# Layer b's projection: gates beside z columns, last weights in a used buffer, sample preparation and position part moved into other stages

## The chip, the core and the metric

The kernel runs on one core of a Trainium2 chip. TensorE (PE; its weight loads are PEld), VectorE (DVE), ScalarE (ACT) and GpSimd (POOL) each run an instruction list written for them and meet at semaphores; SyncE (SP) issues the DMA transfers. The metric is device microseconds of one launch: 1354.34 us before, the median of 3 runs (1353.39 to 1355.47).

## The reference, cut to what matters

The model is a decoder step of two layers, a (dilated attention) and b (native sparse attention), for 512 prompt tokens and 8 x 4 = 32 sample tokens. The change lies in layer b's projection and in the compression of the prompt's keys and values:

```python
def project_b(h, w_in, q_gain, k_gain, pos):
    u = jnp.einsum('ntd,de->nte', h, w_in)          # 1024 -> 3632 columns
    q = rms_norm(u[..., :WIDTH_B]..., q_gain)       # 1024 columns
    kv = u[..., WIDTH_B:o1]...                      # 1536 columns
    gates = jax.nn.sigmoid(u[..., o1:o1 + 3 * HEADS_B]...)   # 48 columns
    z = u[..., o1 + 3 * HEADS_B:]                   # 1024 columns

def compress_rows(x, pe, w1, w2):
    proj = jnp.einsum('ncjkd,rjde->rncke', chunks, w1r)
    hid = jnp.einsum('jd,jde->e', pe, w1)           # the position part: one vector of 128 for k, one for v
    for r in range(CMP_RATIO):
        hid = hid + proj[r, :, r:r + n_cmp]
    return jnp.einsum('ncke,ed->nckd', jax.nn.silu(hid), w2)
```

All data is float32; a matmul of the kernel stands in the trace as two PE instructions.

## The kernel before, in words

A stage is a block: each engine has its list, and the next stage starts when all five lists, SP's among them, are through and a barrier has passed. Layer b runs norm, `project_b_stage`, `prepare_sample_b_stage`, `compress_prompt_stage`, `attend_b_stage`, then the samples.

`project_b_stage` goes through `cols`, eight groups c of weight columns: 0 and 1 are q, 2 to 4 keys and values, 5 the 48 gate columns, 6 and 7 z. For each group there are five units: four tiles of 128 prompt tokens, and the 32 samples. A prompt unit is 8 matmuls over K (L1247), with the tokens as the 128-wide weights and the group's columns streamed. A sample unit (L1244) packs four 32-wide weight loads side by side on the array, each with a quarter of the columns; the gate group has its samples in one plain pass of 32 rows. Units rotate over three PSUM banks; ACT and DVE take them out. After the unit three later, `turn` (L1218 to L1224) transposes a unit's q or keys.

The weights have two slots in `W`: group c lies in slot c % 2, and SP loads group c + 2 when group c is through (L1178). Behind each such load SP issues two copies of sample caches from HBM to HBM (L221), 1 MB and 4 MB. `plain` and `rot` hold normed and rotated q until they are transposed; after group 1 nothing uses them. After group 6, SP issues the weights of the compression (L1577 to L1581) into slot 0.

`prepare_sample_b_stage` then copies the samples' q into a padded tile `T.q` (L1966, 64 small copies on DVE, after POOL cleared it), their keys, values and z into `T` (ACT), stores the samples' gates to HBM and loads them back in another layout (L1911, L1921: eight transfers of 4-byte elements), loads the prompt's key and value rows back as pages (L1916, into slot 1), and computes the position part: 32 matmuls with 128-wide weights from `w1` and a single streamed column (L1938), of which DVE copies the result to `pe_hid` (L1971).

`compress_prompt_stage` works in steps. PE transposes pages (`turn`, L1424), DVE and ACT copy half of each out, then 16 matmuls (`hidden`, L1439, four quarters between the next transposes), SiLU with `pe_hid` as bias (`silu`, L1503), the second weights (`tokens`, L1454) and a norm of the keys. There is one PSUM bank for `turn`, so each waits for both copies of the one before, and one for `hidden`: its second half waits for the first half's SiLU.

Of the kernel before, what the change touches and what calls it, by code (L numbers as in the profile page):

```python
# [13 lines left out]
P = 128  # L14
# [42 lines left out]
def constants():  # L57
# [61 lines left out]
    for name, a in parts.items():  # L119
# [8 lines left out]
            "pa_w0", "pa_w1", "pb_w0", "pb_w1", "cmp_w", "cp_pages0", "cs_pages0", "cs_pages1", "oa_w", "ob_w"]  # L128
# [993 lines left out]
def project_b_stage(S, hT, W, QP, KT, ROWS, WINR, Z, GATES, T_rows, T_z, weights):  # L1122
# [8 lines left out]
    cols = [(0, 512), (512, 512), (1024, 512), (1536, 512), (2048, 512), (2560, NG), (2560 + NG, 512), (3072 + NG, 512)]  # L1131
    NC = len(cols)
    units = []
    for c in range(NC):
        for t in range(TILES + 1):
# [7 lines left out]
            u.R = (2 * NS if u.kv else NS if c == 5 else P) if u.s else P  # L1143
# [3 lines left out]
    with ExitStack() as ctx:  # L1147
# [10 lines left out]
        plain = sb("plain", [P, 3, 512])  # L1158
        rot = sb("rotated", [P, 3, 512])
        s_w = [S.lasting_sem(f"pb_w{i}") for i in range(2)]  # L1160
# [8 lines left out]
        with S.block() as block:  # L1169
            @block.sync  # L1170
            def _(sp):
                for i, name in enumerate(("b_q_norm", "b_k_norm")):
                    sp.dma_start(gains[:, i, :], A[name].broadcast_to((P, DH))).then_inc(s_gains, 16)
                for c in range(NC):
                    if c + 2 < NC:
                        lo, n = cols[c + 2]
                        sp.wait_ge(s_u, 5 * (c + 1))
                        sp.dma_start(W[:, c % 2, :, 0:n], w[:, :, lo:lo + n]).then_inc(s_w[c % 2], 16)  # L1178
                        copy_kept(S, sp, 3, [c])
                        copy_kept(S, sp, 2, [c])  # L1180
# [21 lines left out]
                S.outs += [(S.s_rows_out, 64), (s_win_out, 64), (s_srows_out, 12 * 16)]  # L1202
                sp.wait_ge(s_u, 5 * (NC - 1))
                load_compress_weights(S, sp, weights)

            @block.tensor
            def _(pe):
# [18 lines left out]

                def columns(u, k, j):
                    w_k = W[:, u.c % 2, k, :]
                    if u.kv:
                        return w_k[:, j * P:(j + 1) * P]  # L1230
                    return w_k.rearrange("p (k g d) -> p g k d", k=2, g=GQA)[:, j]
                for u in units:
                    n = cols[u.c][1]
                    if u.t == 0:
                        pe.wait_ge(s_w[u.c % 2], 16 * (u.c // 2 + 1))
                    if u.v >= 3:
                        old = units[u.v - 3]
                        pe.wait_ge(s_n if old.qk else s_lin, old.i + 1)
                        if old.kv:
                            pe.wait_ge(s_v, old.i - 9)  # L1240
                    for k in range(KC):
                        if u.s and u.c != 5:
                            for j in range(4):
                                ins = nc.tensor.matmul(U[u.v % 3][j * NS:(j + 1) * NS, 0:P], hT[:, k, SEQ:TOK], columns(u, k, j),  # L1244
                                                       start=(k == 0), stop=(k == KC - 1), skip_group_check=True)
                        else:
                            ins = nc.tensor.matmul(U[u.v % 3][0:u.R, 0:n], hT[:, k, u.t * P:u.t * P + u.R], W[:, u.c % 2, k, 0:n],  # L1247
                                                   start=(k == 0), stop=(k == KC - 1))
                    ins.then_inc(s_u, 1)
# [4 lines left out]
            def _(act):  # L1254
# [12 lines left out]
                for u in units:  # L1267
# [14 lines left out]
                    elif u.c == 5:  # L1282
                        nc.scalar.activation(GATES[0:u.R, u.t, :], src[0:u.R, 0:n], ACT.Sigmoid).then_inc(s_lin, 1)
                    else:
                        dst = Z[:, u.t % TILES, (u.c - 6) * 512:(u.c - 5) * 512]
                        if u.s:
                            nc.scalar.activation(T_z[:, u.c - 6, :], src[:, 0:P], ACT.Silu).then_inc(s_lin, 1)
                        else:
                            nc.scalar.activation(dst.rearrange("p (g k d) -> p k g d", g=GQA, d=DH),
                                                 src[:, :].rearrange("p (k g d) -> p k g d", g=GQA, d=DH), ACT.Silu).then_inc(s_lin, 1)  # L1290
# [4 lines left out]
            def _(pool):  # L1295
                for u in qk_units:
# [29 lines left out]
            def _(dve):  # L1326
# [45 lines left out]
                second(qk_units[-1])  # L1372

# [520 lines left out]
def prepare_sample_b_stage(S, QP, KT, T_rows, T_z, GATES, T, weights, pages):  # L1894

    nc, A = S.nc, S.dram  # L1900
# [637 lines left out]
```

## Time and profile before

| | us |
|---|---|
| median of 3 runs | 1354.34 |
| profiled execution: its own time | 1350.71 |
| profiled execution: span, first to last instruction | 1348.9 |
| PE busy in the span | 1222.2 (91%) |
| projection of layer b, gate group, four prompt tiles and samples | 722.3 to 735.5 |
| projection, two z groups | 735.5 to 796.1 |
| preparation of the samples, with the position part | 796.1 to 812.1 |
| compression of the prompt | 812.1 to 835.4 |

Times in the trace are counted from the start of the span. In rows of the timeline the columns are start, duration from the first start to the last end of the merged instructions, engine, line, operation, output and inputs, count, and in brackets the idle time just before and what ended it. In tables by stretch, PEclk is the granted TensorE clock: 1.00 is 2.4 GHz, 0.50 is 1.2 GHz.

### The profile page before, as it was taken

What the parts mean: (1) busy time and instruction counts of PE and PEld (TensorE: products, weight loads), DVE (VectorE), ACT (ScalarE), POOL (GpSimd) and SP (SyncE); (2) the same over time, 40 slices, a digit from 0 to 9 for tenths busy, and PEclk for the clock granted to TensorE, in tenths of its full rate; (3) what the DMA queues carried; (4) which work ended last, traced back from release to release, by engine and by line L of the source; (5) the groups of instructions that cost most, each with busy time, mean ns of one, the idle gap of its engine ahead of it and who ended that gap; (6) DMA issues with size and microseconds to landing.
All of it is one profiled execution on the core that took longest, in us unless ns stands there. A gap on an engine that the chain in (4) does not pass through costs nothing. (4 is left out here: it accounts for less than half of the span.)

```text
span 1348.9 us, 20946 instructions
## 1 busy us (share of the span) xinstructions
PE 1222.2 (91%) x7869; PEld 792.6 (59%) x7869; DVE 463.0 (34%) x1205; ACT 394.1 (29%) x947; POOL 295.5 (22%) x423
## 2 busy tenths in 40 slices
PE   3999999999898889699999997999988879797898
PEld 2576576677687743355446465565557767585543
DVE  1333333000455521244121013666742343434321
ACT  5111111111566400512112013666643333333210
POOL 1455554000000000167232001554530000000000
PEclk9999999999999989799998986999989989898999
DMA  6034334582312996336677932302026847343801
GB/s 234 30 147 165 158 136 180 195 290 98 99 44 80 303 295 182 127 125 218 244 230 283 297 55 73 112 2 63 1 58 177 203 125 189 116 135 99 214 9 59
DMA packets 87646, 197.21 MB, mean 146 GB/s; under 512 B 9770, under 2 KB 39258, under 8 KB 86394
## 3 DMA queue, kind: packets, MB, share of 16 engines
q1 hardware_dynamic: 87546, 195.87, 45.7%
q8 instruction: 63, 1.03, 0.3%
q14 instruction: 37, 0.30, 0.1%
HBM read 185.16 MB, written 73.28 MB: 192 GB/s over the span
## 5 line engine op out<-in xcount | busy, mean ns | idle before, releaser
L446 PE MATMUL bank<-la_region,la_hT 128*128 128x512 f32 x640 | 283.2, 599 | 1.7 <-PEq L164 1.7
L446 PEld LDWEIGHTS bank<-la_region,la_hT 128*128 128x128 f32 x640 | 173.1, 275 | 96.2 <-issue 46.7
L1247 PE MATMUL bank<-lb_region,lb_oT 128*128 128x512 f32 (+2 forms) x528 | 210.2, 558 | 2.1 <-PEq L164 1.7
L1247 PEld LDWEIGHTS bank<-lb_region,lb_oT 128*128 128x128 f32 (+1 forms) x528 | 96.5, 199 | 104.4 <-issue 103.3
L1439 PE MATMUL bank<-cs_chunks_turned,lb_region 128*128 128x252 f32 x512 | 125.9, 392 | 4.7 <-ACT cs_hidden L1503 3.9
L1439 PEld LDWEIGHTS bank<-cs_chunks_turned,lb_region 128*128 128x128 f32 x512 | 96.0, 197 | 18.9 <-issue 5.7
L1492 DVE COPY cs_chunks_turned<-bank 64x512 f32<-64x512 f32 x64 | 43.7, 683 | 97.1 <-PE bank L1424 97.1
L1494 ACT ACTIVATE cs_chunks_turned<-bank 64x512 f32<-64x512 f32 x64 | 38.0, 593 | 114.4 <-PE bank L1424 114.3
L494 POOL TENSOR_TENSOR pa_swapped<-pa_normed,pa_tables 128x256 f32<-128x256 f32 (+1 forms) x60 | 50.2, 856 | 77.3 <-DVE pa_normed L513 77.3
L1828 POOL TENSOR_SCALAR ab_probs<-ab_probs,ab_rec,lb_gates 128x128 f32<-128x128 f32 (+3 forms) x96 | 58.2, 623 | 33.8 <-DVE ab_rec L1874 33.6
L465 ACT ACTIVATE pa_squares<-bank 128x512 f32<-128x512 f32 (+1 forms) x30 | 16.0, 533 | 162.4 <-PE bank L446 154.8
L1535 POOL TENSOR_SCALAR cs_ms<-cs_ss 63x4 f32<-63x4 f32 x8 | 1.5, 186 | 252.7 <-DVE cs_ss L1546 252.7
L2233 PE MATMUL bank<-lb_region,lb_oT 128*128 128x512 f32 x128 | 55.9, 595 | 0.0
L1723 PE MATMUL bank<-lb_kT,lb_qp 64*128 64x512 f32 (+3 forms) x256 | 53.6, 497 | 1.4 <-PEq L164 1.1
L1798 ACT ACTIVATE ab_probs<-ab_probs,ab_low 128x128 f32<-128x128 f32 (+3 forms) x96 | 52.6, 551 | 0.0
L484 POOL TENSOR_TENSOR pa_rstd<-pa_mean_square,consts 128x8 f32<-128x8 f32 (+1 forms) x30 | 51.0, 1699 | 2.5
L1275 ACT ACTIVATE pb_squares<-bank 128x256 f32<-128x256 f32 (+3 forms) x25 | 10.8, 431 | 130.6 <-PE bank L1247 125.3
L1860 DVE CUSTOM_DVE_ANT_0 ab_probs<-bank,consts 128x128 f32<-128x128 f32 (+3 forms) x96 | 43.0, 486 | 16.6 <-PE bank L1723 16.6
L687 POOL TENSOR_TENSOR la_z<-la_z,aa_rec 128x512 f32<-128x512 f32 x4 | 4.2, 1043 | 187.7 <-DVE aa_rec L702 187.7
L505 DVE TENSOR_REDUCE pa_square_sum<-pa_squares 128x8 f32<-128x512 f32 (+1 forms) x30 | 18.1, 603 | 72.7 <-ACT pa_squares L465 72.7
L2233 PEld LDWEIGHTS bank<-lb_region,lb_oT 128*128 128x128 f32 x128 | 24.0, 190 | 30.2 <-issue 30.2
L1676 ACT ACTIVATE lb_region<-bank 128x512 f32<-128x512 f32 (+3 forms) x64 | 27.8, 434 | 47.1 <-PE bank L1734 46.9
(334 smaller groups left out, 1808.1 us busy)
## 6 DMA issues: line engine op xcount, KB each, us to landing
la_region<-in_a_w_in SPq DMA_DIRECT2D x10, 2048.0 KB, 8.0
out_new_dil_s<-in_cache_dil SPq DMA_DIRECT2D x8, 2032.0 KB, 13.5
lb_region<-in_b_w_in SPq DMA_DIRECT2D x7, 2048.0 KB, 9.0
la_region<-in_cache_dil SPq DMA_DIRECT2D x13, 1024.0 KB, 15.8
lb_qp<-in_cache_nsa_paged SPq DMA_DIRECT2D x32, 256.0 KB, 4.7
lb_region<-in_cache_nsa_paged SPq DMA_DIRECT2D x32, 256.0 KB, 4.0
sb_sel_keys<-in_cache_nsa_paged SPq DMA_DIRECT2D x64, 128.0 KB, 3.8
sb_sel_values<-in_cache_nsa_paged SPq DMA_DIRECT2D x64, 128.0 KB, 4.1
```

What stands on the lines that cost most here:

```text
L446: ins = nc.tensor.matmul(U[u.v % 3][:, :], permuted(hT[:, k, :], u.g, u.t), W[:, u.c % 2, k, :], start=(k == 0), stop=(k == KC - 1))
L484: nc.gpsimd.tensor_tensor(rstd[:, i % 2, 0:H], ms[:, 0:H], S.const("half_power")[:, 0:H], ALU.pow).then_inc(s_rstd, 1)
L494: nc.gpsimd.tensor_tensor(o3[:, :, lo:lo + HALF], n3[:, :, HALF - lo:DH - lo], tab, ALU.mult).then_inc(s_sw, 1)
L1247: ins = nc.tensor.matmul(U[u.v % 3][0:u.R, 0:n], hT[:, k, u.t * P:u.t * P + u.R], W[:, u.c % 2, k, 0:n], start=(k == 0), stop=(k == KC - 1))
L1439: ins = nc.tensor.matmul(self.hid_bank[:, 0:KVH * nb], self.w1[:, kv, off, mm, :], self.chunksT[:, y % 2, :, mm, off:off + nb], start=(rm ...
L1492: nc.vector.tensor_copy(dst, src).then_inc(self.s_ev[0], 1)
L1494: nc.scalar.activation(dst, src, ACT.Copy).then_inc(self.s_ev[1], 1)
L1723: nc.tensor.matmul(SC[u][:, 0:b.N], QP[b.j][part, 1, g, own_q], KT[part, 1 if b.win else 0, b.j, 0:b.N], start=True, stop=True).then_inc(s ...
L1798: nc.scalar.activation(slots[i][:, 0:b.N], slots[i][:, 0:b.N], ACT.Exp, bias=low[:, i:i + 1], scale=-1.0, accum_out=den[:, i:i + 1]).then_ ...
L1828: nc.gpsimd.tensor_scalar(slots[i][:, 0:b.N], slots[i][:, 0:b.N], rec[:, i:i + 1], GATES[:, b.t, at:at + 1], ALU.mult, ALU.mult).then_inc( ...
L1860: nc.vector.tensor_tensor_reduce(slots[i][:, 0:b.N], SC[u][:, 0:b.N], S.const("causal")[:, (TILES - 1 - b.t) * P:], -SCALE, 3e38, ALU.add, ...
L2233: ins = nc.tensor.matmul(B[6 + v % 2][:, :], oT[:, k, t * P:(t + 1) * P], W_out[:, k, half * 512:half * 512 + 512], start=(k == 0), stop=( ...
```

## The change

The gate group takes the first 256 z columns with it (304 columns), group 6 has 512 z columns, group 7 the last 256. Group 7's weights (1 MB) go into the memory of `plain` and `rot`, which are now one tile, and are issued with group 5's, two groups earlier than before. Slot 1 is thus free after group 5, and the pages are loaded into it from there. The preparation stage is gone: clearing of `T.q`, its copies, the copies of keys and values, and the round trip of the gates stand in the projection's lists; the transposes of z and the position part stand in the compression's. The position part now has the 32-wide broadcast column as weights and streams `w1`'s 128 columns, for k and v side by side on the array; the result lies in rows and is copied, transposed and copied again.

```diff
-    cols = [(0, 512), (512, 512), (1024, 512), (1536, 512), (2048, 512), (2560, NG), (2560 + NG, 512), (3072 + NG, 512)]
+    cols = [(0, 512), (512, 512), (1024, 512), (1536, 512), (2048, 512), (2560, NG + 256), (2816 + NG, 512), (3328 + NG, 256)]
...
+        both = sb("plain_and_rotated", [P, 6, 512])
+        plain, rot = both[:, 0:3, :], both[:, 3:6, :]
+        W_last = both[:, 0:4, :].rearrange("p a b -> p (a b)").rearrange("p (k e) -> p k e", k=KC)
...
+                        if c + 2 < NC - 1:
+                            lo, n = cols[c + 2]
+                            sp.dma_start(W[:, c % 2, :, 0:n], w[:, :, lo:lo + n]).then_inc(s_w[c % 2], 16)
+                        if c == 3:
+                            lo, n = cols[NC - 1]
+                            sp.wait_ge(s_tr, 10)
+                            sp.dma_start(W_last[:, :, :], w[:, :, lo:lo + n]).then_inc(s_w_last, 16)
...
+                sp.wait_ge(s_u, 5 * (NC - 2))
+                sp.wait_ge(S.s_rows_out, 16 * TILES)
...
+                    sp.dma_start(pages0[lo:lo + 64, b // 2, :, :], rows[b, :, :, 0:512]).then_inc(S.lasting_sem("cp_pages0"), 16)
+                sp.wait_ge(s_lin, 5)
+                sp.dma_start(A["scratch_gates"], GATES[0:NS, TILES, :]).then_inc(s_gs, 16)
                 sp.wait_ge(s_u, 5 * (NC - 1))
                 load_compress_weights(S, sp, weights)
+                sp.wait_ge(s_gs, 16)
...
+                        sp.dma_start(T.gates[64 * n2:64 * n2 + 64, pair, :],
+                                     A["scratch_gates"][r:r + NT].rearrange("t (b h) -> h t b", b=3),
+                                     allow_slow_non_contiguous=True).then_inc(s_gl, 16)
+                sp.wait_ge(s_gl, 16 * NB)
...
+                    if u.s and u.c == 5:
+                        for k in range(KC):
+                            ins = nc.tensor.matmul(U[u.v % 3][0:NS, P:P + NG], hT[:, k, SEQ:TOK], weight_rows(u, k)[:, 0:NG],
+                                                   start=(k == 0), stop=(k == KC - 1), skip_group_check=True)
...
+                        functions = ["gates"] * (u.c == 5) + ["z"]
+                        for f in functions if u.t % 2 == 0 else functions[::-1]:
...
+                    if u.c == 6 and u.s:
+                        act.wait_ge(s_ev, 20)
+                        nc.scalar.activation(T.kT[:, :, :, :], KT[:, :, :, SEQ:TOK], ACT.Copy)
...
+                nc.gpsimd.memset(T.q[:, :, :, :, :, :, :], 0.0).then_inc(s_zero, 1)
...
+                                nc.vector.tensor_copy(T.q[part, var, n, j, k2, :, :],
+                                                      QP[j][part, var, :, SEQ + n * NT:SEQ + (n + 1) * NT]).then_inc(s_q, 1)
+                dve.wait_ge(s_q, 8 * NB)
...
-def prepare_sample_b_stage(S, QP, KT, T_rows, T_z, GATES, T, weights, pages):
...
+                for j in range(2):
+                    ins = nc.tensor.transpose(ZB[:, j * P:(j + 1) * P], T_z[:, j * P:(j + 1) * P], ident)
+                ins.then_inc(s_zt, 1)
+                pe.wait_ge(S.lasting_sem("cmp_w"), 16 * 8)
+                nc.tensor.transpose(PB[:, 0:32], pe_rows[:, :], ident[0:32, 0:32])
+                nc.tensor.transpose(PB[:, 128:256], gains[:, :, :].rearrange("p a d -> p (a d)"), ident).then_inc(s_pet, 1)
+                C.pe_step(pe, 0)
+                pe.wait_ge(s_petc, 2)
+                for rm in range(16):
+                    for kv in range(2):
+                        ins = nc.tensor.matmul(HB_[kv * NS:(kv + 1) * NS, 0:HID], peT[:, 16 * kv + rm:16 * kv + rm + 1].broadcast_to((P, NS)),
+                                               w1[:, kv, rm // 8, rm % 8, :], start=(rm == 0), stop=(rm == 15), skip_group_check=True)
+                ins.then_inc(s_ph, 1)
+                C.pe_step(pe, 1)
+                pe.wait_ge(s_phc, 1)
+                nc.tensor.transpose(ZB[:, 256:256 + 2 * NS], hid_rows[:, :], ident[0:2 * NS, 0:2 * NS]).then_inc(s_pht, 1)
...
+                for x in range(4, 8):
+                    C.copy_out(act, x, 1)
+                act.wait_ge(s_pre, 1)
+                C.silu(act, 0)
...
+                C.dve_step(dve, 0)
+                dve.wait_ge(s_ph, 1)
+                nc.vector.tensor_copy(hid_rows[:, :], HB_[0:2 * NS, 0:HID]).then_inc(s_phc, 1)
+                C.dve_step(dve, 1)
+                dve.wait_ge(s_pht, 1)
+                nc.vector.tensor_copy(pe_hid[:, :], ZB[:, 256:256 + 2 * NS:NS]).then_inc(s_pre, 1)
```

SP's list from the last cache copies of the projection (`out_new_win_s`, `out_new_dil_s`) to the end of the preparation; `in_b_cmp_w` is the compression's weights, `out_new_rows_p` into `lb_region` the pages, `lb_s_gates` the samples' gates. Before:

```order
99 L221 DMA out_new_win_s<-in_cache_nsa_win 16x16256
100 L221 DMA out_new_dil_s<-in_cache_dil 64x16384
101 L1577 DMA lb_region<-in_b_cmp_w 64x16x128 x4
102 L1578 DMA lb_w<-in_b_cmp_w 128x2x64
103 L1579 DMA lb_pe_rows<-in_b_cmp_pe 32x128
104 L1581 DMA lb_k_gains<-in_b_k_norm 128x64 x2
105 L160 UNCONDITIONAL_BRANCH
106 L1909 UNCONDITIONAL_BRANCH
107 L1911 DMA scratch_gates<-lb_gates 32x48
108 L1916 DMA lb_region<-out_new_rows_p 64x2x512 x4
109 L1921 DMA lb_s_gates<-scratch_gates 64x3x1 x8
```

And now:

```order
99 L221 DMA out_new_win_s<-in_cache_nsa_win 16x16256
100 L221 DMA out_new_dil_s<-in_cache_dil 64x16384
101 L1215 DMA lb_region<-out_new_rows_p 64x2x512 x4
102 L1217 DMA scratch_gates<-lb_gates 32x48
103 L1642 DMA lb_region<-in_b_cmp_w 64x16x128 x4
104 L1643 DMA lb_w<-in_b_cmp_w 128x2x64
105 L1644 DMA lb_pe_rows<-in_b_cmp_pe 32x128
106 L1646 DMA lb_k_gains<-in_b_k_norm 128x64 x2
107 L1224 DMA lb_s_gates<-scratch_gates 64x3x1 x8
108 L160 UNCONDITIONAL_BRANCH
```

The pages and the store of the gates moved ahead of the compression's weights; the eight loads of the gates stand behind them, at the end of the projection's list (the branch ends a stage's list).

PE's list from the last groups of the projection into the compression; a x8 row is one prompt unit (8 matmuls), the 32-wide rows are the samples. Before, from the gate group on:

```order
297 L1247 MATMUL bank<-lb_region,lb_oT 128x48 x8
298 L1247 MATMUL bank<-lb_region,lb_oT 32x48 x8
299 L1247 MATMUL bank<-lb_region,lb_oT 128x512 x32
300 L1244 MATMUL bank<-lb_region,lb_oT 32x128 x32
301 L1247 MATMUL bank<-lb_region,lb_oT 128x512 x32
302 L1244 MATMUL bank<-lb_region,lb_oT 32x128 x32
303 L160 UNCONDITIONAL_BRANCH
304 L1926 UNCONDITIONAL_BRANCH
305 L1929 MATMUL bank<-consts,lb_s_z 128x128 x2
306 L1933 MATMUL bank<-consts,lb_pe_rows 128x32
307 L1934 MATMUL bank<-consts,lb_k_gains 128x128
308 L1938 MATMUL bank<-lb_peT,lb_region 128x1 x32
```

And now, from the last z groups on:

```order
292 L1282 MATMUL bank<-pb_plain_and_rotated,lb_oT 128x256 x32
293 L1279 MATMUL bank<-pb_plain_and_rotated,lb_oT 32x64 x32
294 L160 UNCONDITIONAL_BRANCH
295 L2400 UNCONDITIONAL_BRANCH
296 L2404 MATMUL bank<-consts,lb_s_z 128x128 x2
297 L2407 MATMUL bank<-consts,lb_pe_rows 128x32
298 L2408 MATMUL bank<-consts,lb_k_gains 128x128
299 L1489 MATMUL bank<-consts,lb_region 128x128 x8
300 L2413 MATMUL bank<-lb_region,lb_peT 32x128 x32
301 L1504 MATMUL bank<-cp_chunks_turned,lb_region 128x124 x4
```

One stage's end is gone, group 7 streams half as many columns, and the position part (L2413) stands between the first four transposes of pages (L1489, two pages each) and the first quarter of `hidden` (L1504).

## Rows read from the trace of the kernel before

**Rows 1.** Table by stretch of all engines; columns: stretch, length, busy times (instructions), PEclk, DMA.

```profile
core 0: us, PE busy (x) PEld busy (x) DVE busy (x) ACT busy (x) POOL busy (x), PEclk, DMA share, GB/s
722.30:735.50 13.20, 12.83 (x88) 12.05 (x87) 2.77 (x8) 3.95 (x12) 4.16 (x9) 0.70 1.09 397
...
766.10:796.10 30.00, 29.65 (x132) 13.76 (x128) 0.00 (x0) 2.95 (x6) 0.00 (x0) 1.00 0.46 75
796.10:812.10 16.00, 13.58 (x69) 13.15 (x69) 6.08 (x67) 1.80 (x6) 0.95 (x1) 0.60 0.34 68
812.10:835.40 23.30, 15.64 (x98) 13.44 (x99) 4.44 (x11) 4.53 (x13) 1.21 (x3) 0.72 0.00 1
```

**Rows 2.** Timeline, PE: sample units, gate units, a quarter of the samples' hidden part.

```profile
720.25 1.69 PEld L1244 LDWEIGHTS bank<-lb_region,lb_oT 128*32 128x32 f32 x64 [0.17 <-issue]
...
724.42 1.99 PE L1247 MATMUL bank<-lb_region,lb_oT 128*128 128x48 f32 x16
...
727.01 3.12 PE L1247 MATMUL bank<-lb_region,lb_oT 128*128 128x48 f32 x16 [0.37 <-DVE pb_normed L1344]
...
793.80 1.95 PE L1244 MATMUL bank<-lb_region,lb_oT 128*32 128x128 f32 x64
...
1055.69 1.87 PE L1439 MATMUL bank<-cs_chunks_turned,lb_region 128*128 128x252 f32 x8
```

**Rows 3.** Table by stretch of all engines, cut where the granted clock changes.

```profile
727.60:737.40 9.80, 9.80 (x49) 8.35 (x49) 0.28 (x1) 2.13 (x5) 0.13 (x1) 0.50 1.05 392
...
796.00:798.40 2.40, 1.16 (x7) 0.79 (x7) 0.62 (x8) 1.57 (x7) 0.95 (x1) 1.00 0.02 3
798.40:822.60 24.20, 20.68 (x97) 19.14 (x97) 7.96 (x67) 2.60 (x8) 0.00 (x0) 0.52 0.22 45
822.60:833.50 10.90, 7.00 (x64) 6.37 (x62) 1.66 (x4) 1.98 (x6) 1.19 (x2) 0.97 0.01 2
```

**Rows 4.** Timeline of the preparation stage.

```profile
797.95 5.97 DVE L1966 COPY lb_s_q<-lb_qp 64x16 f32<-64x16 f32 x64
...
798.09 12.72 PE L1938 MATMUL bank<-lb_peT,lb_region 128*128 128x1 f32 x64 [0.35 <-DVE lb_k_gain L1958]
...
799.77 6.47 SPq L1921 DMA_DIRECT2D lb_s_gates<-scratch_gates  x8
810.92 0.16 DVE L1971 COPY lb_pe_hidden<-bank 128x2 f32<-128x2 f32 x1 [7.00 <-PE bank L1938]
```

**Rows 5.** Timeline of the compression stage.

```profile
812.09 0.66 PE L1424 MATMUL bank<-consts,lb_region 128*128 128x128 f32 x2 [1.28 <-PEq L164]
...
816.97 2.04 PE L1439 MATMUL bank<-cp_chunks_turned,lb_region 128*128 128x124 f32 x8 [0.56 <-DVE cp_chunks_turned L1492]
...
823.35 1.05 PE L1439 MATMUL bank<-cp_chunks_turned,lb_region 128*128 128x124 f32 x8
...
834.33 0.28 DVE L1558 TENSOR_SCALAR lb_kc_p<-bank,lb_k_gain 128x62 f32<-128x62 f32 x1 [1.73 <-PE bank L1464]
```

**Rows 6.** Timeline, SP's issues at the projection's end.

```profile
735.90 9.07 SPq L221 DMA_DIRECT2D out_new_win_s<-in_cache_nsa_win  x1
...
766.26 6.01 SPq L1577 DMA_DIRECT2D lb_region<-in_b_cmp_w  x4
...
775.83 0.90 SPq L1581 DMA_DIRECT2D lb_k_gains<-in_b_k_norm  x2
```

**Rows 7.** SP's waits, 560 to 840; columns: total us, times, longest.

```profile
SPq L160 <- DMA lb_s_gates<-scratch_gates: 1.8, 1, 1.8
```

**Rows 8.** Table by stretch of the DMA engines; columns: stretch, length, PEclk, DMA share, GB/s.

```profile
718.00:722.20 4.20, 1.00 0.02 4
722.20:764.50 42.30, 0.88 1.02 370
...
768.00:780.00 12.00, 1.00 1.12 184
```

**Rows 9.** DMA issues, 722 to 722.6: count, KB, us from issue to landing.

```profile
lb_region<-in_b_w_in SPq DMA_DIRECT2D x1, 2048.0 KB, 7.8
```

More of the change, by code:

```diff
@@ L1142, in project_b_stage @@
             u.heads = (2 if u.s else 8) if u.q else (2 if u.s else 4)
-            u.R = (2 * NS if u.kv else NS if c == 5 else P) if u.s else P
+            u.R = 2 * NS if u.s and u.kv else P
             u.ri = u.i if c < 2 else u.i - 5
@@ new lines, in _ @@
+                    if u.c == 6 and u.s:
+                        act.wait_ge(s_ev, 20)
+                        nc.scalar.activation(T.kT[:, :, :, :], KT[:, :, :, SEQ:TOK], ACT.Copy)
+                        act.wait_ge(s_v, 15)
+                        for which in range(2):
+                            for j in range(2):
+                                nc.scalar.activation(T.v[:, which, j * P:(j + 1) * P], T_rows[(2 + j) * NS:(3 + j) * NS, 1 + which, :],
+                                                     ACT.Copy)
@@ L1372, in _ @@
                 second(qk_units[-1])
+                dve.wait_ge(s_zero, 1)
+                dve.wait_ge(s_ev, 10)
+                for var in range(2):
+                    for j in range(2):
+                        for k2 in range(2):
+                            part = slice(k2 * DH, (k2 + 1) * DH)
+                            for n in range(NB):
+                                nc.vector.tensor_copy(T.q[part, var, n, j, k2, :, :],
+                                                      QP[j][part, var, :, SEQ + n * NT:SEQ + (n + 1) * NT]).then_inc(s_q, 1)
+                dve.wait_ge(s_q, 8 * NB)
 class Compress:
@@ L2398, in _, with compress_prompt_stage @@
                 interleave((scores, least, weights, turns, output, merge), lambda y: C.dve_step(dve, y), unit, rest)
-def compress_prompt_stage(S, KC_P, VC_P, weights, pages):
+def compress_prompt_stage(S, KC_P, VC_P, weights, pages, T_z, T):
+    nc = S.nc
     s_pg = [S.lasting_sem("cp_pages0")]
+    w1, _, pe_rows, peT, pe_hid, gains, gain = weights
+    s_zt, s_pet, s_petc, s_ph, s_phc, s_pht, s_pre = (
+        S.sem("pp_" + n) for n in ("z_turned", "turned", "copied", "hidden", "hidden_copied", "hidden_turned", "hidden_done"))
+    ZB, PB, HB_ = S.banks[3:6]
     def landed(pe, it, s_pg):
@@ L2415, in _ @@
             def _(act):
-                for y in range(C.last):
+                act.wait_ge(s_zt, 1)
+                nc.scalar.activation(T.zT[:, :], ZB[:, 0:2 * P], ACT.Copy)
+                C.act_step(act, 0)
+                for x in range(4, 8):
+                    C.copy_out(act, x, 1)
+                act.wait_ge(s_pre, 1)
+                C.silu(act, 0)
+                for y in range(2, C.last):
                     C.act_step(act, y)
@@ L2424, in _ @@
             def _(dve):
-                for y in range(C.last):
+                dve.wait_ge(s_pet, 1)
+                nc.vector.tensor_copy(peT[:, :], PB[:, 0:32]).then_inc(s_petc, 1)
+                nc.vector.tensor_copy(gain[:, :], PB[:, 128:129]).then_inc(s_petc, 1)
+                C.dve_step(dve, 0)
[4 more added lines that the diff above has]
+                nc.vector.tensor_copy(pe_hid[:, :], ZB[:, 256:256 + 2 * NS:NS]).then_inc(s_pre, 1)
+                for y in range(2, C.last):
                     C.dve_step(dve, y)
```

142 lines of the change are left out of this document (47 added, 95 removed).

## The prediction

> **What bounds the kernel now.** I read the table by stretch first [rows 1], cut at the stages that the change touches. In the z groups PE is busy 29.65 of 30.00 us at the full clock (1.00, 2.4 GHz), so there only fewer or shorter PE instructions help. The gate group before them takes 13.20 us at a mean clock of 0.70, though it streams a tenth of the columns. The preparation stage takes 16.00 us and the compression 23.30 us, at 0.60 and 0.72. Nothing of another stage lies beside them, since each stage ends at a barrier, so what leaves this stretch leaves the total, unless another list of the same stage ends late.
>
> Second, the timeline of these stages. A gate unit of 16 instructions takes 1.99 us at the full clock, 0.12 us for one, and 3.12 us where the clock has fallen [rows 2]; the clock stood at 0.50 (1.2 GHz) from 727.6 to 737.4, after some 5 us of these short units, and came back in the 512-column units that followed [rows 3]. In the preparation PE's 64 one-column instructions (798.09 to 810.81) are the longest list and DVE's copy at 810.92 waits for them; DVE's 64 copies and SP's eight gate loads lie beside them [rows 4]. SP's list ends 1.8 us after its last gate issue [rows 7], at 808.1, so it was nearly as late. In the compression the clock is still at 0.52 until 822.6 [rows 3].
>
> **The change, part by part.** The profiled execution took 1350.71 us (span 1348.9), the median of the runs is 1354.34; I sum in the trace's time and take the difference off the median.
>
> *The three groups.* A 512-column instruction costs (29.65 - 1.95) / 64 = 0.433 us [rows 1, 2]. In proportion 304 columns cost 0.257 and 256 cost 0.216; a 252-column row gives 1.87 / 8 = 0.234 with the last one's run-out in it [rows 2], which would make 304 columns 0.28. I take the proportional ones, and hold 1.5 us a group for the other end. Weight loads, 0.12 us a piece at most, hide under them. Group 5: 64 x 0.257 = 16.4, the transposes of keys between its units about 0.9 (three pairs, of which one takes 0.66 us at half clock [rows 5], and a small one), the samples' z 1.7 and their gates 0.8 (below the 1.95 of the 128-column sample unit and half of a 48-column unit's 16 instructions at 1.99): 19.8, so it ends at 742.1 instead of 735.5. With no unit that short, the fall of the clock there goes too. Group 6 costs 29.7 as a z group does now and ends at 771.8. Group 7: 64 x 0.216 + 1.7 = 15.5, PE's end at 787.3 against 795.75.
>
> *Group 7's weights and the pages.* Their 1 MB and group 5's extra 1 MB go out at group 3's end; the DMA engines stand empty from 718.0 to 722.2 (4 GB/s) [rows 8], which takes in half of it. Group 6's weights land 7.8 us after their issue at 722.3 [rows 9]; even 4 us later that is 734, eight us ahead of need. No cost. Free of slot 1's reuse, the copies and pages queued at 742 replace group 7's 2 MB of before by 1 MB of pages, so the queue that was empty at 764.5 should be about as early; the need is at 771.8.
>
> *The preparation's pieces.* DVE's copies (5.97 us [rows 4]) fall into groups 5 and 6, where DVE does next to nothing (0.28 us busy in 9.80 from 727.6 on [rows 3]), ACT's five into 30 us where it is busy 2.95 [rows 1], POOL's clearing (0.95 us) in front of the first unit. More function-table loads on ACT come with mixed gates and z, under a 4.3 us unit of PE. All at nothing; that cover is many us wide.
>
> *SP's list is late next.* The weights of the compression are issued at group 6's end: 766.26 to 776.73 now, 10.5 us [rows 6]; from 771.9 that is 782.4. Behind them, no longer in a stage of their own, stand the eight gate loads: 6.47 us [rows 4] to 788.9, and 1.8 us to the last landing [rows 7]: 790.7. That is 3 us after PE and ACT (787.3 + 0.4), and the stage ends with it. A stage's end costs 0.9 us (834.6 to the next stage's first instruction at 835.4, 811.1 to 812.1), so the compression starts at 791.6, not 812.09 [rows 5]: 20.5 us less. If the gate issues were slow only because pages moved beside them, they end up to 3 us sooner; if SP is late, everything behind moves with it.
>
> *The compression gets longer.* Ahead of the first page come four transposes, 1.1 us (1.2 us from the stage's start to the position part now [rows 4]). The position part, 64 instructions of 128 columns with 32-wide weights, has no row of its own. Nearest is the sample unit, 64 of the same size in four streams, 1.95 us [rows 2]; here only two streams run, 3.9 us at the full clock and 7.8 at half. From the other side, one stream only: the 124-column instructions cost 2.04 / 8 = 0.25 us at half and 1.05 / 8 = 0.13 at full clock [rows 5], 64 of them 16.3 or 8.4 us. I take two streams, since the four of the sample unit plainly overlap. The clock: it fell by 798.4, 2.6 us after the last long matmul, with PE half idle between [rows 3], and PE will have stood some 4 us at SP's wait, so the stage starts at half clock as now. It came back at 822.6, 5.7 us after PE became dense with `hidden` at 816.94 [rows 3, 5]; counted from the position part's start that does 5.7 / 7.8 of it at half, the rest at full: 6.7 us. It fills the 0.6 us in which PE waits for the fourth copy. From then the three quarters of `hidden` that run at 2.04 us go at 1.05 [rows 5]: 2.8 us less. The copy, transpose and copy of the result stand ahead of the first SiLU, which PE's second half waits for: 0.3 us. Sum: 1.1 + 6.7 - 0.6 - 2.8 + 0.3, and 0.4 for two changes of the array's form (PEld idles 0.17 us ahead of a sample unit [rows 2]) = 5.1 us.
>
> The Trainium skill speaks against a part packed in this way: "TensorEngine Tiling (Array Packing)", Key Properties, says that changing the tiling mode drains TensorE. Without a drain the sum would be 0.4 us lower; the gap of 0.17 us in the trace agrees with one. The same section says that tiles work independently, four of 128 x 32; the position part uses two, and by that rule too it takes twice the sample unit's 1.95 us; a run at that form alone is not in the trace.
>
> Total: -20.5 + 5.1 = -15.4 us. In the profiled time 1335.3; against the median 1354.3 - 15.4 = 1338.9. What follows the compression only shifts: its first transfers are issued by its own stage.
>
> **Rivals.**
>
> *Earlier (20%).* The gate loads end with PE, or PE's clock survives the wait. For it: the issues shared the queue with pages. Against: 6.47 us for eight looks like the issue itself. With the stage's end at 787.7 + 0.9 and full clock: -23.5 us, and the compression's extra is 0.9 + 3.9 - 0.6 - 2.8 - 1.1 (four turns at full clock) + 0.7 = 1.0: 1331.8.
>
> *The position part runs in one stream (15%).* For it: each matmul is two instructions on the same columns, one after the other. Against: the sample unit's are too. 5.7 us at half clock does 23 instructions, 41 more at 0.13 take 5.3: 11.0, 4.3 us more, 1343.2; with the clock at half throughout 16.3, and no 2.8 back: 1351.
>
> *The queue is late, and the end slower (10%).* SP's list is one order: cache copies, pages, gates' store, weights, gates. SP was held 9.07 us at a copy [rows 6]. The copies ran at 370 GB/s, the weights' small pieces at 184 [rows 8]. At 742 some 3 MB of earlier copies and stores (6 MB less 8 us at 370 GB/s), 5 MB of new ones and 1 MB of pages are ahead. At 370 that is 24 us, to 766. At 184, with pages and copies mixed, it is 49 us, to 791; the 18.8 us of weights and gates behind would end the stage at 810, and the compression, 5.1 us longer, would end 4 us later than now: 1358. It turns into a loss when the queue empties after 787. The Trainium skill has the rule behind this, "DMA: Bandwidth & Descriptors", Queues, rings and completion order: on each DMA engine descriptors are consumed in ring order, so a late head delays all behind it. No row shows pages and copies mixed. I give 5% to a loss of 5 to 13 us (1344 to 1351), 2% to no change, 3% to slower.
>
> **How the numbers follow.** The forecast, SP last and half clock at the compression's start, has 55%: 1338.9, with 1335.5 to 1342 as its own range. Earlier 20%, one stream 15%, queue 10%. About 0.2% (2.7 us) is what a measurement of this kernel can tell from no change. Faster 0.95, same 0.02, slower 0.03. The range 1331.0 to 1346.5 leaves out about 1 in 10 above and less below.
>
> **What would show it.** The gate group some 20 us at clock 1.00; group 7's first unit right behind group 6; no list of DVE or ACT at the stage's end, but SP's wait for the gates there, with PE idle 3 to 5 us; the first page's transposes near 792; the position part 6 to 7 us, its 64 instructions 0.06 us apart at full and 0.12 at half clock; `hidden` at 1.05 a quarter; the attention's start near 820. It is wrong if PE waits for group 6's weights, if the weights' issue starts late, or if the position part takes 10 us or more.

## The result, and the profile after

The changed kernel takes 1333.69 us, the median of 4 runs (1330.71 to 1336.62), against 1353.90 (1353.39 to 1355.47) for the kernel before, measured with it. The ratio is 0.9849 [0.9822, 0.9875]: 20.2 us, or 1.5%, less. The forecast was 1338.9 in a range from 1331.0 to 1346.5. The profiled execution took 1336.62 us with a span of 1334.8.

I compare one stretch in all kernels: from the first matmul of the gate group's first unit to the first matmul of the attention. It holds everything of PE that the change touches. Before it is 722.41 to 835.42, 113.0 us; after it is 724.09 to 818.94, 94.85 us. The clock that the stretch leaves behind still acts in the attention, so run 5 adds a second mark some 13 us further on.

The table by stretch of the changed kernel, cut at its groups and where the clock changes, with the columns of [rows 1]:

```profile
724.00:743.10 19.10, 19.10 (x152) 14.10 (x151) 8.45 (x72) 10.05 (x18) 4.15 (x9) 1.00 1.07 381
743.10:772.60 29.50, 29.50 (x130) 13.75 (x128) 0.00 (x0) 4.51 (x13) 0.00 (x0) 1.00 0.77 254
772.60:787.80 15.20, 15.15 (x132) 13.02 (x128) 0.00 (x0) 3.24 (x10) 0.00 (x0) 1.00 0.90 148
788.00:792.00 4.00, 0.65 (x4) 0.45 (x5) 0.00 (x0) 0.24 (x2) 0.00 (x0) 0.97 0.06 2
792.00:801.90 9.90, 8.22 (x61) 6.05 (x63) 1.92 (x6) 1.70 (x5) 0.00 (x0) 0.50 0.00 1
801.90:818.90 17.00, 11.52 (x107) 10.42 (x103) 3.21 (x9) 3.00 (x8) 1.18 (x3) 0.90 0.00 1
```

The three groups run at 1.00 throughout; before, the gate group alone had a mean of 0.70 [rows 1]. Then PE stands still, the clock falls at about 792 and is back at 801.9. The 0.90 of the last stretch is a second fall, at 815.6.

The timeline of PE, the rows that answer to [rows 2, 4, 5]:

```profile
724.09 4.26 PE L1282 MATMUL bank<-lb_region,lb_oT 128*128 128x304 f32 x16
...
741.40 1.10 PE L1279 MATMUL bank<-lb_region,lb_oT 128*32 128x64 f32 x64
742.31 0.84 PE L1286 MATMUL bank<-lb_region,lb_oT 128*32 128x48 f32 x16
...
786.65 1.10 PE L1279 MATMUL bank<-pb_plain_and_rotated,lb_oT 128*32 128x64 f32 x64
791.35 0.41 PE L2404 MATMUL bank<-consts,lb_s_z 128*128 128x128 f32 x2 [3.60 <-PEq L164]
...
796.41 6.38 PE L2413 MATMUL bank<-lb_region,lb_peT 128*32 128x128 f32 x64
802.72 1.16 PE L1504 MATMUL bank<-cp_chunks_turned,lb_region 128*128 128x124 f32 x8
...
818.94 2.08 PE L1788 MATMUL bank<-lb_kT,lb_qp 64*128 64x512 f32 x4 [1.19 <-PEq L164]
```

PE ends the projection at 787.75 and waits 3.60 us at the barrier. Whom it waits for, SP's timeline (with DVE's copies, now ahead of it) and SP's waits show; they answer to [rows 4, 6, 7]:

```profile
729.74 5.97 DVE L1435 COPY lb_s_q<-lb_qp 64x16 f32<-64x16 f32 x64
...
743.19 0.58 SPq L221 DMA_DIRECT2D out_new_win_s<-in_cache_nsa_win  x1
...
772.77 5.04 SPq L1642 DMA_DIRECT2D lb_region<-in_b_cmp_w  x4
777.85 3.03 SPq L1643 DMA_DIRECT2D lb_w<-in_b_cmp_w  x1
...
782.55 5.12 SPq L1224 DMA_DIRECT2D lb_s_gates<-scratch_gates  x8
```

```profile
SPq L160 <- DMA lb_s_gates<-scratch_gates: 2.7, 1, 2.7
```

The gate loads are issued until 787.67 and SP waits another 2.7 us for the last one: 790.4, 0.95 us ahead of the next stage's first instruction. SP is the last list, as forecast.

### The profile page after: what moved, and what is told of

The parts are those of the page before. It is cut to its first block and busy times, and to the rows that moved or that the text cites. A ratio compares the mean times of both kernels' runs of the same rounds, so it can differ in the third digit from the quotient of the medians.

```text
span 1334.8 us, 21066 instructions
## 1 busy us (share of the span) xinstructions
PE 1210.1 (91%) x7934; PEld 790.2 (59%) x7934; DVE 463.7 (35%) x1206; ACT 400.1 (30%) x960; POOL 296.0 (22%) x423
## 5 line engine op out<-in xcount | busy, mean ns | idle before, releaser
L1282 PE MATMUL bank<-lb_region,lb_oT 128*128 128x512 f32 (+1 forms) x448 | 187.3, 575 | 1.6 <-PEq L164 1.6
L1282 PEld LDWEIGHTS bank<-lb_region,lb_oT 128*128 128x128 f32 x448 | 84.6, 192 | 92.1 <-issue 88.2
L1504 PE MATMUL bank<-cs_chunks_turned,lb_region 128*128 128x252 f32 x512 | 127.4, 395 | 4.7 <-ACT cs_hidden L1568 3.9
L1504 PEld LDWEIGHTS bank<-cs_chunks_turned,lb_region 128*128 128x128 f32 x512 | 97.0, 199 | 19.1 <-issue 5.7
L494 POOL TENSOR_TENSOR pa_swapped<-pa_normed,pa_tables 128x256 f32<-128x256 f32 (+1 forms) x60 | 50.2, 856 | 77.2 <-DVE pa_normed L513 77.2
L2217 PEld LDWEIGHTS bank<-lb_region,lb_oT 128*128 128x128 f32 x128 | 24.0, 190 | 30.1 <-issue 30.1
## 6 DMA issues: line engine op xcount, KB each, us to landing
la_region<-in_cache_dil SPq DMA_DIRECT2D x13, 1024.0 KB, 15.5
```

The lines of the kernel that those rows point to most:

```text
L494: nc.gpsimd.tensor_tensor(o3[:, :, lo:lo + HALF], n3[:, :, HALF - lo:DH - lo], tab, ALU.mult).then_inc(s_sw, 1)
L1282: ins = nc.tensor.matmul(U[u.v % 3][:, 0:n], hT[:, k, u.t * P:(u.t + 1) * P], weight_rows(u, k), start=(k == 0), stop=(k == KC - 1))
L1504: ins = nc.tensor.matmul(self.hid_bank[:, 0:KVH * nb], self.w1[:, kv, off, mm, :], self.chunksT[:, y % 2, :, mm, off:off + nb], start=(rm ...
L2217: ins = nc.tensor.matmul(B[6 + v % 2][:, :], oT[:, k, t * P:(t + 1) * P], W_out[:, k, half * 512:half * 512 + 512], start=(k == 0), stop=( ...
```

## The experiments

The theory is the forecast's: the merged groups save PE time and clock; the folded preparation saves a stage; SP's list ends it 3 us late; that wait brings the clock down, so the position part runs in two streams at mostly half clock. The rivals: SP is not what holds the stage's end, or the position part runs in one stream or costs its whole length, or one part of the change does all. Kernels 1 to 4 ran on one chip, 5 to 8 on a second, 9 and 10 on a third, each time with the kernel before beside them (1352.01, 1352.47 and 1352.61 us).

**1. Gate loads ahead of the weights.** The gates' store goes to the end of group 5, the eight loads ahead of the wait for group 6 and the weights behind it.

```diff
+                        if c == 5:
+                            sp.wait_ge(s_lin, 5)
+                            sp.dma_start(A["scratch_gates"], GATES[0:NS, TILES, :]).then_inc(s_gs, 16)
...
-                sp.wait_ge(s_u, 5 * (NC - 1))
-                load_compress_weights(S, sp, weights)
...
+                sp.wait_ge(s_u, 5 * (NC - 1))
+                load_compress_weights(S, sp, weights)
```

> The changed kernel with the store of the samples' gates moved ahead of the last cache copies, and their eight loads ahead of the compression's weights. Mark: from the first matmul of the gate group to the attention's first matmul, 113.1 us before and 94.9 changed. Theory, SP's gate loads end the projection 3.3 us after PE: the stage now ends with ACT, the compression starts 2.4 us sooner, the clock still falls at its start since PE idles over a us and then waits on copies: 92.5. Rival, PE's shorter wait keeps the clock at 1.00 through the transposes: the position part takes 3.9 instead of 6.4 us too, 89. Rival, something else ends the stage or the weights now land late: 95, no gain.

Measured: 1330.69 us, ratio to before 0.984 [0.9823, 0.9857]; the stretch is 89.27 us. PE's timeline:

```profile
785.71 1.10 PE L1280 MATMUL bank<-pb_plain_and_rotated,lb_oT 128*32 128x64 f32 x64
787.93 0.41 PE L2405 MATMUL bank<-consts,lb_s_z 128*128 128x128 f32 x2 [1.12 <-PEq L164]
...
792.09 4.73 PE L2414 MATMUL bank<-lb_region,lb_peT 128*32 128x128 f32 x64
```

PE's idle time at the barrier falls from 3.60 to 1.12 us, and the compression starts 64.8 us after the first matmul instead of 67.3. The loads now take 15.2 us to issue, behind the cache copies and the pages, but that lies beside group 6. So SP was last, by 2.5 us. The stretch came out 3.2 us below the 92.5 expected, near the 89 of the first rival, but not by its mechanism: the clock still fell (at 790.9), under the short transposes with 0.56 us gaps, only later, and was back at 794.1, so that the position part took 4.73 us.

**2. The merged groups alone.** The kernel before with the new column groups, `both`, `W_last` and `weight_rows` as in the change; the preparation stage stays.

```diff
-    cols = [..., (2560, NG), (2560 + NG, 512), (3072 + NG, 512)]
+    cols = [..., (2560, NG + 256), (2816 + NG, 512), (3328 + NG, 256)]
...
```

> The kernel before with the changed column groups and the last group's weights in the place of plain and rotated q alone; the preparation stage and the position part stay as before. Same mark. Theory, the groups' share is 9.6 us and independent of the rest: 103.5, about 1344.3 us. Rival, only the loss from the clock's fall in the gate group is saved: 107 to 108. Rival, the two added megabytes of early loads delay group 6's weights or the stores: more than 105, with PE waiting in the trace.

Measured: 1343.63 us, 0.994 [0.9925, 0.9954]; the stretch is 101.55 us, 11.5 less than before. PE's timeline:

```profile
789.53 0.41 PE L1958 MATMUL bank<-consts,lb_s_z 128*128 128x128 f32 x2 [1.09 <-PEq L164]
...
790.72 12.66 PE L1967 MATMUL bank<-lb_peT,lb_region 128*128 128x1 f32 x64 [0.35 <-DVE lb_k_gain L1987]
804.65 0.66 PE L1453 MATMUL bank<-consts,lb_region 128*128 128x128 f32 x2 [1.28 <-PEq L164]
...
809.54 2.04 PE L1468 MATMUL bank<-cp_chunks_turned,lb_region 128*128 128x124 f32 x8 [0.56 <-DVE cp_chunks_turned L1521]
...
811.80 1.39 PE L1468 MATMUL bank<-cp_chunks_turned,lb_region 128*128 128x124 f32 x8
```

The groups take 63.7 us (724.77 to 788.43), the preparation its old 15.1. The preparation starts 64.8 us after the first matmul instead of 74.5, so 9.7 of the 11.5 us are the groups'. The compression is 21.7 us instead of 23.3, for a reason outside the edit: the clock was back in the second quarter (1.39 us), 3.0 us after PE became dense and not 5.7. The medians differ by 8.4 us only.

**3. No position part.** Its 64 instructions, copy, transpose and copy go, and the compression adds zeros in their place.

```diff
-                pe.wait_ge(s_petc, 2)
-                for rm in range(16):
-                    for kv in range(2):
-                        ins = nc.tensor.matmul(HB_[kv * NS:(kv + 1) * NS, 0:HID], ...)
...
+                nc.vector.memset(pe_hid[:, :], 0.0).then_inc(s_pre, 1)
```

> The changed kernel without the position part's 32 matmuls and its copies and transpose; zeros stand in its place, so the compression leaves out that term. Same mark. Theory, the position part costs 6.4 us where it stands but brings the clock back, which three to four quarters of the first half after it need: without it these run at 2.0 instead of 1.1 us, so only some 3.5 us go: 91.3. Rival, the quarters are fast for another reason: all 6.5 us go, 88.4.

Measured: 1333.39 us, 0.9861 [0.9845, 0.9878], no faster in the median than the change with it; the stretch is 91.20 us. The quarters of `hidden`:

```profile
796.74 2.04 PE L1504 MATMUL bank<-cp_chunks_turned,lb_region 128*128 128x124 f32 x8 [0.56 <-DVE cp_chunks_turned L1557]
...
799.00 1.91 PE L1504 MATMUL bank<-cp_chunks_turned,lb_region 128*128 128x124 f32 x8
...
801.12 1.43 PE L1504 MATMUL bank<-cp_chunks_turned,lb_region 128*128 128x124 f32 x8
...
802.61 1.05 PE L1504 MATMUL bank<-cp_chunks_turned,lb_region 128*128 128x124 f32 x8
```

The first three quarters run slow, since now they are what brings the clock back. Of the 6.4 us that the position part fills, only 3.65 leave the stretch (1.55 against its second profile in run 5). It pays for the clock that `hidden` then uses, which was the forecast's "2.8 us less".

**4. Position part with k and v one after the other.** The same instructions with the loops exchanged, so that neighbours use the same column tile of the array.

```diff
-                for rm in range(16):
-                    for kv in range(2):
+                for kv in range(2):
+                    for rm in range(16):
```

> The changed kernel with the position part's loops exchanged: all of k, then all of v, so that neighbouring instructions write the same rows of the bank. Same mark. Theory, k and v overlap as two streams because they alternate: now one after the other, 26 instructions at 0.21 us until the clock rises 5.5 us after the start, then 38 at 0.107: 9.6 instead of 6.4 us, 98. Rival, the order does not matter (each instruction is as fast alone): 95.

Measured: 1336.27 us, 0.9882 [0.9865, 0.9898]; the stretch is 97.70 us. The table by stretch of this line alone (busy PE, PEld; PEclk), cut where the clock rose:

```profile
795.60:799.60 4.00, 3.98 (x19) 3.34 (x20) 0.50 0.00 0
799.60:804.20 4.60, 4.60 (x47) 4.44 (x45) 1.00 0.01 4
```

That is 8.69 us instead of 6.38, though the clock was back after 4.0 us and not 5.5: 0.21 us an instruction at half clock, 0.098 at full.

**5. The changed kernel again**, beside the next three.

> The changed kernel once more, beside the others on one chip. From the first matmul of the gate group to the attention's first: 94.9 us before this run's clock is known. Theory, the clock returns at no fixed time after PE becomes dense (2.0, 3.0, 4.0, 5.6, 5.7 us in the profiles so far), so the stretch moves by up to 2 us from run to run: 93 to 95.5. Rival, it is fixed by the kernel: 94.9 within 0.2.

Measured: 1333.04 us, 0.9865 [0.9849, 0.9881]; the stretch is 92.75 us, 2.1 shorter than in its first profile and just under the 93 to 95.5 expected. The position part alone, by stretch:

```profile
795.10:797.70 2.60, 2.60 (x26) 2.24 (x28) 0.50 0.00 0
797.70:799.90 2.20, 2.20 (x42) 2.04 (x38) 1.00 0.00 0
```

It took 4.94 us, since the clock was back after 2.6 us of it and not 5.5. One instruction takes 0.10 us at half clock and 0.052 at full, half of what run 4 shows: two streams it is. That is 1.4 of the 2.1 us; another 0.6 lies at the stretch's end, where in the first profile the clock had fallen at 815.6. But most of the 2.1 us is paid back in the attention. I take as a second mark the first 16 instructions of its line L1830 (L1765 before); the rows are of the kernel before, of the changed kernel's first profile and of this run:

```profile
848.24 1.95 PE L1765 MATMUL bank<-lb_region,lb_rows 128*64 128x256 f32 x16
...
823.42 3.01 PE L1788 MATMUL bank<-lb_kT,lb_qp 64*128 64x128 f32 x12 [0.54 <-DVE ab_low L1925]
831.71 1.95 PE L1830 MATMUL bank<-lb_region,lb_rows 128*64 128x256 f32 x16
...
820.16 4.82 PE L1788 MATMUL bank<-lb_kT,lb_qp 64*128 64x128 f32 x12 [0.30 <-DVE ab_low L1925]
829.88 1.95 PE L1830 MATMUL bank<-lb_region,lb_rows 128*64 128x256 f32 x16
```

The clock is back 3.5 us after the attention's first matmul in the first profile and 9.4 in this one. Counted to this second mark the change takes 107.6 and 107.0 us against 125.8 before: 18.2 and 18.8 less.

**6. Run 1 again.**

> The kernel with the gates' loads moved ahead, once more. The first profile gave 89.3 us for the stretch: 2.5 us from the earlier stage and 3.1 from the clock, which fell 3 us after the stage began and came back 2.0 us after the position part began. Theory, the 2.5 us belong to the kernel and come again, the rest is the clock's phase: 89 to 92.5, the compression starting 64.7 to 64.9 us after the first matmul. Rival, the shorter wait is what kept the clock: 89.3 within 0.5.

Measured: 1328.40 us, 0.9834 [0.9814, 0.9853]; the stretch is 91.11 us. The clock fell at 789.0 here and was back at 795.8 (in run 1 it fell at 790.9 and was back at 794.1). Against the changed kernel on the same chip that is 4.6 us in the medians, of which 2.5 are SP's. To the second mark both profiles of this kernel take 103.5 us, 3.5 to 4.1 less than the change, though their stretches differ by 1.8.

**7. Run 1 with the position part in four quarters**, each behind one of the first four transposes, so that PE has work while their copies run.

```diff
-                C.pe_step(pe, 0)
-                pe.wait_ge(s_petc, 2)
-                for rm in range(16):
-                    for kv in range(2):
+                for x in range(4):
+                    C.turn(pe, x)
+                    if x == 0:
+                        pe.wait_ge(s_petc, 2)
+                    for rm in range(4 * x, 4 * x + 4):
+                        for kv in range(2):
```

> The kernel with the gates' loads moved ahead, and the position part cut in four quarters of 16 instructions, one behind each of the first four transposes of pages, where PE waits for the copies. Theory, each quarter (0.9 us at the full clock, 1.7 at half) fills the 0.6 us wait, and PE is dense from the stage's start, so that the clock stays or comes back sooner: the first quarter of the hidden part starts 6 us after the stage, not 8.8, and the stretch is 86 to 87. Rival, the clock falls all the same: 2.4 us a turn, 10.5 us to the hidden part, 90 to 91. Rival, the copies on DVE and ACT set the pace and nothing is hidden: 89 to 90.

Measured: 1325.87 us, 0.9807 [0.9793, 0.9822]; the stretch is 87.27 us. PE's timeline:

```profile
788.62 0.41 PE L2405 MATMUL bank<-consts,lb_s_z 128*128 128x128 f32 x2 [1.12 <-PEq L164]
...
789.81 1.07 PE L2416 MATMUL bank<-lb_region,lb_peT 128*32 128x128 f32 x16
790.81 0.44 PE L1490 MATMUL bank<-consts,lb_region 128*128 128x128 f32 x2
791.18 1.07 PE L2416 MATMUL bank<-lb_region,lb_peT 128*32 128x128 f32 x16
...
794.91 1.16 PE L1505 MATMUL bank<-cp_chunks_turned,lb_region 128*128 128x124 f32 x8
...
797.01 0.38 PE L1490 MATMUL bank<-consts,lb_region 128*128 128x128 f32 x2
797.23 1.05 PE L1505 MATMUL bank<-cp_chunks_turned,lb_region 128*128 128x124 f32 x8
```

Almost no wait is left between the stage's start and `hidden`, 6.3 us (6 were expected), and all of it runs at full clock. Of the changed kernel's 11.4 us (791.35 to 802.72) that takes away the copies' waits and the half clock at once.

**8. The folded preparation alone.** The change with the column groups of before; slot 1 is then in use until the end, and the pages come after group 7, last on SP's list.

```diff
-    cols = [..., (2560, NG + 256), (2816 + NG, 512), (3328 + NG, 256)]
+    cols = [..., (2560, NG), (2560 + NG, 512), (3072 + NG, 512)]
...
-                sp.wait_ge(s_u, 5 * (NC - 2))
...
+                sp.wait_ge(s_u, 5 * NC)
```

> The changed kernel with the column groups of before (48, 512, 512), group 7's weights in slot 1 again; the samples are still prepared inside the projection and the position part stands in the compression. The pages can then be loaded only when group 7 is through. Theory, freeing slot 1 is what lets the stage go: PE waits for the pages until some 7 us after the compression's start, and the stretch is 107 of 113 before, so that the parts alone (11.5 or 9.6, and 6) give less than both (18). Rival, the pages' load is hidden and the parts simply add: 102 to 103.

Measured: 1346.88 us, 0.9961 [0.9947, 0.9975]; the stretch is 107.40 us, 5.6 less than before. PE's timeline:

```profile
799.56 0.66 PE L2382 MATMUL bank<-consts,lb_s_z 128*128 128x128 f32 x2 [3.91 <-PEq L164]
...
802.94 0.69 PE L1467 MATMUL bank<-consts,lb_region 128*128 128x128 f32 x2 [2.07 <-DMA lb_region<-out_new_rows_p]
...
807.22 6.36 PE L2391 MATMUL bank<-lb_region,lb_peT 128*32 128x128 f32 x64
```

SP is last again, now with the pages (issued 795.72 to 798.22), and then PE waits 2.07 us for the first one. The 107 expected came out, but by other parts: the first transpose of a page comes 3.4 us after the stage's start, not 7, and the stage starts 77.2 us after the first matmul, later than the preparation before it (74.5). In the changed kernel the merge frees slot 1 two groups early, and PE waits for no page.

**9. Run 7 with the gate loads late**, in the changed kernel's place: the quarters alone.

> The changed kernel with only the position part interleaved with the transposes; the gates' loads stand at the projection's end as in the change, so PE idles some 3.6 us before the stage. Theory, the short wait and the dense start together kept the clock: it fell 2.6 to 4.4 us after PE's last long matmul in every profile in which PE was not dense again 1.2 us later, so it falls here at the stage's start and comes back 2 to 6 us after; the quarters run at 1.7 us first, and the stretch is 91 to 93. Rival, being dense from the stage's start is enough: the clock stays at 1.00, the quarters take 1.07 us, 89.8.

Measured: 1331.50 us, 0.9841 [0.9828, 0.9855]; the stretch is 91.72 us. The table by stretch, as above:

```profile
788.30:791.30 3.00, 0.00 (x0) 0.00 (x0) 0.00 (x0) 0.22 (x1) 0.00 (x0) 1.00 0.11 9
791.30:798.10 6.80, 6.29 (x42) 4.14 (x42) 1.09 (x4) 1.15 (x3) 0.00 (x0) 0.50 0.00 1
798.10:816.36 18.26, 12.73 (x128) 11.21 (x126) 4.05 (x11) 3.79 (x11) 1.22 (x3) 0.97 0.00 1
```

After 3.5 us without work the clock falls in spite of the dense PE behind, and two of the quarters take 1.92 us. So in these profiles the short wait alone (runs 1 and 6) did not keep the clock, nor did the dense work alone (here); both together did (runs 7 and 10). Whether any work without gaps would do is open: in run 2 an idle 1.09 us, three short steps and 0.35 us more stood ahead of the old position part, single streamed columns without a gap, and the clock fell at 792.0, 1.3 us into it. To the second mark the quarters alone save 1.0 to 1.6 us (106.0), behind the early loads 3.6 to 3.9 (99.9 and 99.7 in runs 7 and 10 against run 1's 103.5).

**10. Run 7 again**, beside run 9.

> The kernel with both the gates' loads ahead and the position part interleaved, once more, beside the other. Theory, its clock at 1.00 from the projection's end to the end of the hidden part belongs to the kernel: 87.3 within 0.5 again. Rival, the first profile was a lucky phase: the clock falls in the first turns, 88.5 to 90.

Measured: 1325.45 us, 0.9802 [0.9786, 0.9818]; the stretch is 86.85 us. The table by stretch, as above:

```profile
785.30:788.70 3.40, 2.15 (x73) 1.57 (x72) 0.32 (x3) 1.09 (x4) 0.00 (x0) 1.00 0.03 7
788.70:793.80 5.10, 5.10 (x71) 3.81 (x71) 1.57 (x4) 1.42 (x4) 0.00 (x0) 1.00 0.00 0
```

The clock stays at 1.00 across the barrier, as in run 7. This kernel is faster than the kernel before and than the changed one: 27.2 us below the kernel before (26.6 in run 7), and 7.2 us below the changed kernel on run 5's chip (1325.87 against 1333.04, with no overlap of the single runs).

## Why the prediction was right

It was right in its direction and mechanism; its time was 5.2 us above the measured 1333.69, which lies inside the whole range but under the 1335.5 to 1342 that the forecast gave its own story, and nearer to the rival "Earlier" (1331.8). The trace shows the forecast's story and not that rival's: the gate loads ended after PE, PE stood still for 3.60 us, and the clock fell. The sizes were off, most of them to the same side. The steps in turn, counted from the first matmul of the stretch where a time is meant (722.3 in the forecast, 724.09 in the trace):

- *The three groups.* Forecast PE's end after 65.0 us, measured 63.66. Group 5 took 19.0 for 19.8, group 6 29.55 for 29.7, group 7 15.1 for 15.5. The proportional price of 304 columns was the right choice: 4.31 us from unit to unit, of which 0.2 are the transposes between, against 16 x 0.257 = 4.1. The samples' z of 64 columns, put at 1.7 us below the row of 128 columns, took 0.91 (741.40 to 742.31) and 1.10: that is the 1.3 us by which the sum was high. Run 2 shows these groups with the old preparation: 63.7 us again.
- *Clock in the gate group.* Forecast to stay, and it stays at 1.00. That is a part of the step above, not a gain beside it.
- *Weights and pages early, copies on DVE and ACT, all at nothing.* DVE's 64 copies take their 5.97 us from 729.74 on, beside PE's group 5; ACT ends at 788.0, 0.3 us after PE. No unit waits for weights; SP issues the two copies of 743.19 in 0.6 us each where it was held 9.07 before [rows 6], so the third rival, the late queue, fell.
- *SP is late next.* Forecast stage start after 69.3 us, measured 67.3; run 1 shows by its 2.5 us that this is what sets it. The terms were high: weights 9.74 for 10.5, gates 5.12 for 6.47. The last landing took 2.7 for 1.8. The forecast's doubt about the gate issues was justified: 0.64 us each (5.10 for eight in runs 5 and 8 too), 0.81 in [rows 4]. That pages moved beside them there is not shown to be the reason: the DMA engines moved 119 GB/s beside the issues in both.
- *The compression gets longer.* Forecast +5.1, measured 27.6 against 23.3, +4.3. The position part took 6.38 for 6.7 in the first profile, but 4.94 in run 5. Two streams held (runs 4 and 5 together), at 0.052 us an instruction at full clock and 0.10 at half, where 0.061 and 0.122 were taken. The three quarters of `hidden` went from 6.38 us to 3.43, 2.95 less for 2.8. A loss of 0.5 us was not in the sum: the second weights ran at half clock from 815.6 on (1.03 us for 0.61). The term that has no one value is how long the clock stays down: I took 5.7 us from the one row of before [rows 3]. That matches the first profile (5.5), which is luck, and is more than twice that of run 5 (2.6).
- *The array's form.* I took 0.4 us for two changes. In run 7, 16 position instructions follow one another to the next transpose in 1.00 us, where 16 x 0.052 is 0.84; and from transpose to position part are 0.37 us, to `hidden` 0.22. So I estimate a change of form at some 0.15 us, 0.3 for two; no run has the same instructions without the change. It agrees with what the Trainium skill says in "TensorEngine Tiling (Array Packing)", Key Properties, that a change of mode drains the engine; the drain itself no row shows.

The stretch lost 18.2 us in the first profile and 20.3 in run 5, where 15.4 were forecast; of the 2.8 us beyond it in the first, 1.9 come from the groups and SP and 0.8 from the compression. By parts: merge alone 11.5, folding alone 5.6, both 18.2 to 20.3. Runs 2 and 8 do not quite add up to it, and in the medians the gap is wider: 8.4 and 5.6 against 19.4 to 20.2. Run 8 shows the waits that the folding pays without the merge (SP's for the pages, then PE's 2.07 us); that they are the whole gap is an argument and not shown by a run of its own.

What stays open is the rest of the median's gain. The program outside the stretch took 1235.9 us in the profile of before and 1236.5 to 1242.4 in the eleven profiles after it, with no order by what was edited. Up to 1.8 us of that spread is the attention's start at half clock: from its first matmul to the second mark are 12.4 to 12.8 us in nine of the twelve profiles and 14.3 in runs 1, 5 and 9. The rest has no cause shown. The profiled execution of before, at 1350.71 us, was also 1.3 to 3.6 us below its medians, so differences of single profiles miss those of medians by a few us.

## What to carry to other kernels

When a stage is folded into the one before it, write down what each queue issues last: here eight transfers of 4-byte elements stood behind the big ones on SP and held a stage by 2.5 us, though all engines were done. Small transfers that are ready early go in front of large ones that must wait. A wait and the clock are one price: where PE comes out of a wait, put independent dense work between the short steps that follow. In runs 7 and 10 it filled their gaps and, behind a wait of 1.12 us, the clock stayed up. And when a change moves the clock, set the end mark behind the stage that follows: what the clock gave in one stage was in part taken back in the next.

## What the runs showed of the hardware that was not expected

- The time that the clock stays low after PE becomes dense is not fixed: 5.7 us before [rows 3, 5], 5.5 and 2.6 in two profiles of the changed kernel, 2.0 and 4.2 in two of run 1's, 3.0 in run 2, 5.2 in run 3, 4.0 in run 4, 5.5 in run 8. For one kernel this moves the stretch by 2 us, but the second mark by at most 0.6.
- Behind an idle 1.12 us the clock fell in both profiles with transposes and 0.56 us gaps (runs 1 and 6) and in neither with dense work (runs 7 and 10). Behind an idle 1.09 us, three short steps and 0.35 us more it fell too, under single-column instructions without a gap (run 2).
- The order of the instructions decides whether column tiles overlap: alternating k and v 0.10 us each at half clock and 0.052 at full, one after the other 0.21 and 0.098.
- An issue of the small gate loads costs SP 0.64 us behind the compression's weights, 0.81 behind the pages [rows 4] and 15.2 / 8 = 1.9 behind cache copies and pages (run 1). What sets it is not shown: at 0.64 and at 0.81 the DMA engines moved 119 GB/s, at 1.9 they moved 287.
